# A two-block network's opening: norm's weight applied in rows through a spread on TensorE, h rounded by tiles of tokens, and x's second tile loaded behind the first weights

## What is computed

```
def rmsnorm(x, g):
    xf = x.astype(jnp.float32)
    y = xf * lax.rsqrt(jnp.mean(xf * xf, axis=-1, keepdims=True) + EPS)
    return (y * g.astype(jnp.float32)).astype(x.dtype)
...
    h = rmsnorm(x, norm_mix_g[l])
    proj = jnp.einsum('bsd,dc->bsc', h, w_in[l])
    u, v, bg, cg, xs, ga, gb = jnp.split(proj, split_at, axis=-1)
    v = rmsnorm(jax.nn.gelu(v, approximate=False), norm_v_g[l])
...
    x = x + conv_ffn(h, ffn_w_up[i], ffn_conv_w[i], ffn_conv_b[i], ffn_w_down[i])
return rms_norm(x, final_norm_g)
```

## Time and profile before

| | |
|---|---|
| median of three runs | 1022.09 us (1021.5 to 1022.81) |
| the profiled execution's own time | 1022.21 us |
| its span | 1020.4 us |
| TensorE busy | 1004.5 us, 98% |
| VectorE busy | 760.2 us, 74% |
| ScalarE busy | 572.8 us, 56% |
| first instruction of TensorE | 4.43 us into the span |

### The profile page before, as it was taken

How to read it: one execution, slowest core, us unless ns; L and a number is a source line. 1 busy time by engine, 2 the same in 40 slices (tenths; PEclk the granted TensorE clock), 3 DMA queues, 4 the chain that set the end, 5 groups by cost and what they waited for, 6 DMA issues and landing times.

```text
span 1020.4 us, 18696 instructions
## 1 busy us (share of the span) xinstructions
PE 1004.5 (98%) x7236; PEld 934.2 (92%) x7236; DVE 760.2 (74%) x1015; ACT 572.8 (56%) x817; POOL 6.6 (1%) x20
## 2 busy tenths in 40 slices
PE   7999999999999999999999999999999999999997
PEld 5999999999999999977899999999998898888886
DVE  7676655557766656787878877778878789888886
ACT  7543444445444445557866555555646675666665
POOL 0000000000000000000000000000020000000000
PEclk9999999999999999999999999999999999999999
DMA  8645556456665664454464666674324574666652
GB/s 301 211 154 176 190 200 203 165 168 203 207 198 173 201 208 167 138 198 140 163 188 125 186 185 186 185 211 142 125 63 103 166 226 139 199 190 191 190 162 83
DMA packets 191265, 178.87 MB, mean 175 GB/s; under 512 B 17444, under 2 KB 169586, under 8 KB 191218
## 3 DMA queue, kind: packets, MB, share of 16 engines
q1 hardware_dynamic: 191218, 178.22, 56.3%
HBM read 177.15 MB, written 1.05 MB: 175 GB/s over the span
## 4 chain that ended last, share of the span: by engine, by line
PE 91%; DVE 5%; ACT 2%; DMA 2%; issue 0%; SPq 0%; DVEq 0%; ACTq 0%
PE psum L622 18%; PE psum L624 17%; PE psum L623 17%; PE psum L824 14%; PE psum L826 7%; PE psum L629 4%; PE psum L631 4%; PE psum L630 4%; DVE whl L1751 2%; DMA raw<-da_w_qkv 1%; PE psum L956 1%; ACT whl L1266 1%; PE psum L972 1%; DMA raw<-w_in 1%; PE psum L1204 1%; DVE stat L2133 1%
## 5 line engine op out<-in xcount | busy, mean ns | idle before, releaser
L1751 DVE TENSOR_TENSOR whl<-raw,whl 128x2048 fp32r<-128x2048 f32 (+2 forms) x145 | 298.1, 2062 | 77.5 <-ACT whl L1266 77.0
L1266 ACT ACTIVATE whl<-raw 128x2048 fp32r<-128x2048 f32 (+2 forms) x145 | 248.1, 1716 | 73.6 <-DMA raw<-w_ff 25.8
L622 PE MATMUL psum<-hT,whl 128*128 128x256 f32 (+1 forms) x784 | 220.4, 281 | 0.9 <-DVE hT L1826 0.9
L623 PE MATMUL psum<-hT,whl 128*128 128x256 f32 (+1 forms) x784 | 219.2, 280 | 0.0
L624 PE MATMUL psum<-hT,whl 128*128 128x256 f32 (+1 forms) x784 | 218.5, 279 | 0.0
L824 PE MATMUL psum<-hT,whl 128*128 128x512 f32 x608 | 212.9, 391 | 0.0
L826 PE MATMUL psum<-hT,whl 128*128 128x256 f32 x608 | 171.4, 282 | 0.0
L622 PEld LDWEIGHTS psum<-hT,whl 128*128 128x128 f32 (+1 forms) x784 | 147.1, 188 | 1.5 <-issue 0.7
L623 PEld LDWEIGHTS psum<-hT,whl 128*128 128x128 f32 (+1 forms) x784 | 147.2, 188 | 0.1
L624 PEld LDWEIGHTS psum<-hT,whl 128*128 128x128 f32 (+1 forms) x784 | 147.2, 188 | 0.0
L622 PE MATMUL psum<-lat,whl 128*128 128x256 f32 (+1 forms) x512 | 144.4, 282 | 0.4 <-DVE whl L1751 0.3
(11 more groups left out here) (250 smaller groups left out, 1582.1 us busy)
## 6 DMA issues: line engine op xcount, KB each, us to landing
raw<-w_ff SPq DMA_DIRECT2D x32, 1024.0 KB, 5.6
raw<-w_in SPq DMA_DIRECT2D x24, 1024.0 KB, 5.1
raw<-ffn_w_up SPq DMA_DIRECT2D x44, 512.0 KB, 4.9
q_sb<-ffn_w_up SPq DMA_DIRECT2D x44, 512.0 KB, 5.0
raw<-da_w_qkv SPq DMA_DIRECT2D x12, 1024.0 KB, 5.0
q_sb<-ffn_w_down SPq DMA_DIRECT2D x22, 512.0 KB, 3.7
raw<-ffn_w_down SPq DMA_DIRECT2D x22, 512.0 KB, 3.6
raw<-w_proj_a SPq DMA_DIRECT2D x4, 1024.0 KB, 5.2
```

The lines of the kernel that those rows point to most:

```text
L622: mm(dst, weight(n, 0, cols, kt, c0, m), hi, start=start, stop=False, skip_group_check=True)
L623: mm(dst, weight(n, 0, cols, kt, c0, m), lo, start=False, stop=False, skip_group_check=True)
L1266: fn(whl[:, slot, 0, 0:w], landing(n)[:, 0:w], ACT.Copy).then_inc(hi_ready, 1)
L1751: tt(whl[:, slot, 1, 0:w], landing(n)[:, 0:w], whl[:, slot, 0, 0:w].bitcast(F32), ALU.subtract).then_inc(lo_ready, 1)
```

## The change

- The weight of the norm is loaded as one row of 1024 (`mix_row`) and spread over all 128 partitions by two fp32 matmuls with a row of ones (`unit_row`), into two PSUM banks. VectorE multiplies it in when it scales the rows (`normal_x`, two products of 512 columns for each tile), so that `round_h` and `rest_h` need no scale.
- TensorE turns the scaled rows tile by tile into two banks for each tile (`h_bank`), and `round_h` and `rest_h` work on four blocks of one tile at a time, in the order tile 0 low half, tile 1 low half, tile 0 high half, tile 1 high half (`H_ORDER`).
- Tile 1's transposes of scaled rows stand behind the first six matmuls of v, and the transposes of x's tile 1 behind tile 0 of the second chunk. The deviation of tile 1 comes behind h of tile 0 on ScalarE and VectorE. The copies of tile 0 into `xT` are now ScalarE's.
- SyncE issues the first half chunk ahead of x's tile 1. The column form of the weight is loaded later with the other vectors.
- In `inject_x` the products with the identity are marked as transposes.

```diff
@@ SyncE
-            sp.dma_start(vec_rows[0:KT, 0, :], a["norm_mix_g"].rearrange("l (r c) -> (l r) c", c=P)).then_inc(mix_landed, 16)
-            sp.dma_start(x_rows[:, 1, :], x_in[:, 1, :]).then_inc(x_landed[1], 16)
+            sp.dma_start(mix_row[:], a["norm_mix_g"]).then_inc(mix_landed, 16)
             for n in range(N_MIX):
...
                 sp.dma_start(dst[:, 0:KT // 4, :], src[:, 0:KT // 4, :]).then_inc(half_landed[n], 16)
+                if n == 0:
+                    sp.dma_start(x_rows[:, 1, :], x_in[:, 1, :]).then_inc(x_landed[1], 16)
                 sp.dma_start(dst[:, KT // 4:, :], src[:, KT // 4:, :]).then_inc(rest_landed[n], 16)
...
-            for name, rows in VEC_ROWS[1:]:
+            for name, rows in VEC_ROWS:
@@ TensorE
+        H_ORDER = [(0, 0), (1, 0), (0, 1), (1, 1)]
+        h_bank = ((py, px), (bank[2], bank[3]))
...
+            def turn_x(dst, src, t, ready, done):
+                for kt in range(KT):
+                    if ready is not None and kt % 4 == 0:
+                        pe.wait_ge(ready, 2 * t + kt // 4 + 1)
+                    last = nc.tensor.transpose(flat(dst[kt // 4])[:, kt % 4 * P:(kt % 4 + 1) * P],
+                                               src[:, t, kt * P:(kt + 1) * P], ident)
+                    if kt % 4 == 3:
+                        last.then_inc(done, 1)
...
+            turn_x(bank[0:2], x_rows, 0, None, x_turned)
+            pe.wait_ge(const_set, 2)
             pe.wait_ge(mix_landed, 16)
+            for half in range(2):
+                last = mm(flat(up[half]), unit_row[:], mix_row[:, half * D // 2:(half + 1) * D // 2], start=True, stop=True)
+            last.then_inc(mix_spread, 1)
+            turn_x(h_bank[0], vtok, 0, xn_ready, xn_turned)
@@ v_rows
+                    if n == 0 and at == 0:
+                        pe.wait_ge(x_read, t + 1)
+                    if n == 1 and t == 1 and at == 0:
+                        pe.wait_ge(x_landed[1], 16)
+                        turn_x(h_bank[0], x_rows, 1, None, x_turned)
                     if t == 0 and at == KT // 4:
+                        if n == 0:
+                            turn_x(h_bank[1], vtok, 1, xn_ready, xn_turned)
                         pe.wait_ge(lo_ready, n + 1)
-                    if t == 0 and n < 2:
-                        pe.wait_ge(h_ready, max(2, kt + 1))
+                    if n < 2:
+                        pe.wait_ge(h_ready, 2 * H_ORDER.index((t, n)) + 2)
@@ inject_x
                             mm(token_sum(t, kt // 4)[:, kt % 4 * P:(kt % 4 + 1) * P], xT[:, kt, t * P:(t + 1) * P], ident,
-                               start=kt % 4 == 0, stop=False, skip_group_check=True)
+                               start=kt % 4 == 0, stop=False, is_transpose=True, skip_group_check=True)
@@ ScalarE
-                fn(hT[:, kt, 0, :], bank[kt // 2][:, kt % 2, :], ACT.Identity, scale=mix_g[:, kt:kt + 1]).then_inc(h_hi, 1)
+            def round_h(t, c):
+                act.wait_ge(xn_turned, 2 * t + c + 1)
+                fn(hT[:, 4 * c:4 * c + 4, 0, t * P:(t + 1) * P], of_tiles(h_bank[t][c]), ACT.Copy).then_inc(h_hi, 2)
...
+            x_deviation(0)
             split_hi_half(0, 0)
+            for half in range(2):
+                act.wait_ge(x_turned, half + 1)
+                fn(xT[:, 4 * half:4 * half + 4, 0:P], of_tiles(bank[half]), ACT.Copy).then_inc(x_read, 1)
+            for at in H_ORDER[0:1]:
+                round_h(*at)
+            x_deviation(1)
+            split_hi_half(0, 1)
+            for at in H_ORDER[1:3]:
+                round_h(*at)
             split_hi_half(1, 0)
+            for at in H_ORDER[3:4]:
+                round_h(*at)
             split_hi_half(1, 1)
@@ VectorE
+            def normal_x(t):
+                dve.wait_ge(x_std, t + 1)
+                step.wait(step.mark(nc.vector.reciprocal(xstat[:, 2, t:t + 1], xstat[:, 1, t:t + 1])))
+                dve.wait_ge(mix_spread, 1)
+                for half in range(2):
+                    cols = slice(half * D // 2, (half + 1) * D // 2)
+                    stt(vtok[:, t, cols], x_rows[:, t, cols], xstat[:, 2, t:t + 1], up[half].rearrange("p a b -> p (a b)"),
+                        ALU.mult, ALU.mult).then_inc(xn_ready, 1)
+            normal_x(0)
             split_lo_half(0, 0)
+            for at in H_ORDER[0:1]:
+                rest_h(*at)
+            normal_x(1)
+            split_lo_half(0, 1)
+            for at in H_ORDER[1:3]:
+                rest_h(*at)
             split_lo_half(1, 0)
+            for at in H_ORDER[3:4]:
+                rest_h(*at)
             split_lo_half(1, 1)
```

More of the change, by code:

```diff
@@ L692, in turn_reciprocal @@
                 last.then_inc(r_turned, 1)
-            pe.wait_ge(ident_landed, 16)
-            pe.wait_ge(mix_landed, 16)
-            nc.tensor.transpose(bank[3][:, 0, 0:KT], vec_rows[0:KT, 0, :], ident[0:KT, 0:KT]).then_inc(mix_turned, 1)
-            x_bank = [up[0], up[1], px, py]
-            def turn_x(dst, src, t, done):
-                for kt in range(KT):
-                    last = nc.tensor.transpose(dst[kt // 2][:, kt % 2, t * P:(t + 1) * P],
-                                               src[:, t, kt * P:(kt + 1) * P], ident)
-                    if done is not None and kt % 2 == 1:
-                        last.then_inc(done, 1)
-            pe.wait_ge(x_landed[0], 16)
-            turn_x(x_bank, x_rows, 0, None)
-            pe.wait_ge(mix_g_read, 1)
-            pe.wait_ge(xn_ready, 1)
-            turn_x(bank, vtok, 0, None)
-            pe.wait_ge(xn_ready, 2)
-            turn_x(bank, vtok, 1, xn_turned)
-            pe.wait_ge(x_landed[1], 16)
-            turn_x(x_bank, x_rows, 1, x_turned)
             def flat(b):
                 return b.rearrange("p a b -> p (a b)")
+            x_bank = [up[0], up[1], px, py]
+            def turn_x(dst, src, t, ready, done):
[6 more added lines that the diff above has]
+                        last.then_inc(done, 1)
+            pe.wait_ge(ident_landed, 16)
+            pe.wait_ge(x_landed[0], 16)
+            turn_x(bank[0:2], x_rows, 0, None, x_turned)
+            pe.wait_ge(const_set, 2)
+            pe.wait_ge(mix_landed, 16)
+            for half in range(2):
+                last = mm(flat(up[half]), unit_row[:], mix_row[:, half * D // 2:(half + 1) * D // 2], start=True, stop=True)
+            last.then_inc(mix_spread, 1)
+            turn_x(h_bank[0], vtok, 0, xn_ready, xn_turned)
             def v_rows(n):
@@ L1318, in _, with x_deviation @@
             x_flat = t_act[:].rearrange("p a b c -> p (a b c)")
-            for t in range(TT):
+            def x_deviation(t):
                 act.wait_ge(x_landed[t], 16)
@@ L1325, in _ @@
                 fn(xstat[:, 1, t:t + 1], xstat[:, 0, t:t + 1], ACT.Sqrt, bias=eps[:, 0:1], scale=1.0 / D).then_inc(x_std, 1)
+            x_deviation(0)
             split_hi_half(0, 0)
-            act.wait_ge(mix_g_read, 1)
-            for kt in range(KT):
-                if kt == KT // 2:
-                    split_hi_half(0, 1)
-                round_h(kt)
+            for half in range(2):
[7 more added lines that the diff above has]
+                round_h(*at)
             split_hi_half(1, 0)
+            for at in H_ORDER[3:4]:
+                round_h(*at)
             split_hi_half(1, 1)
@@ L1814, in split_lo_half, with rest_h @@
                    ALU.subtract).then_inc(half_lo if half == 0 else lo_ready, 1)
-            def rest_h(kt):
-                dve.wait_ge(h_hi, kt // 2 * 2 + 2)
-                stt(hT[:, kt, 1, :], bank[kt // 2][:, kt % 2, :], mix_g[:, kt:kt + 1], hT[:, kt, 0, :].bitcast(F32),
-                    ALU.mult, ALU.subtract).then_inc(h_ready, 1)
+            def rest_h(t, c):
+                dve.wait_ge(h_hi, 2 * H_ORDER.index((t, c)) + 2)
+                four, of_t = slice(4 * c, 4 * c + 4), slice(t * P, (t + 1) * P)
+                tt(hT[:, four, 1, of_t], of_tiles(h_bank[t][c]), hT[:, four, 0, of_t].bitcast(F32),
+                   ALU.subtract).then_inc(h_ready, 2)
             def rest_x(k, c, gain):
@@ L1892, in _ @@
                     split_lo(n)
+                if c == 0:
+                    for half in range(2):
+                        dve.wait_ge(x_turned, 3 + half)
+                        copy(xT[:, 4 * half:4 * half + 4, P:2 * P], of_tiles((py, px)[half])).then_inc(x_read, 1)
             dve.wait_ge(v_std, 1)
```

26 lines of the change are left out of this document (8 added, 18 removed).

## The result

The changed kernel takes 1027.39 us (median of six executions, 1026.76 to 1028.12), the kernel before beside it 1021.8 (1020.37 to 1022.81). The ratio is 1.006, with an interval of 1.005 to 1.0069: slower by some 5.6 us. The forecast was 1022.6 with a range up to 1024.2, so the range missed it by over 3 us.

A forecast was written before the change was run, and what follows sets the result against it. TensorE, busy 98% of the span, was taken to bound the kernel. From a median of 1022.09 us, opening +2.05 and injection -1.55 gave 1022.6 us, range 1021.0 to 1024.2.

The forecast's parts named there:

- The landing: Opening transfers: with the issue order swapped, the first half chunk lands near 7.3 us and x's tile 1 near 8.9.
- The spread: TensorE's opening: two fp32 matmuls of 512 columns, four passes, from 6.15 to 8.87 us; VectorE has the weight at 9.07.
- I take the change of pace at 8.15, as in before: Within the spread: TensorE runs at the slow early pace until 8.15 us, then twice as fast.
- The third rival: Opening: the whole spread runs at the early pace, 3.44 us instead of 2.72, 1.15 more, total 1023.8; chance 0.13.
- VectorE's chain: Behind the spread: two products, first weights' rest, rest of h, done at 12.23; v's first matmuls at 12.31 against 12.29.
- The second wait: After tile 1's transposes: TensorE idles from 14.59 until VectorE's second half chunk's rest, resuming at 15.32, 1.18 us later.
- The rest of the stream: The remaining 90 matmuls of v run unstopped, but x's tile 1 transposes stand inside: 0.87 us; opening 2.05 later.
- Behind it ... all shifts together: After the opening: everything that loads or rounds waits for buffers TensorE frees, so all moves by the same amount.
- The injection: Last stage: 16 transposes replace 32 passes, 1.83 us less, of which a wait for weights takes back 0.28: 1.55 less.
- The fourth rival: Opening: TensorE falls back to the lower clock level, resuming 1.5 us past 15.32, total 1024.4; chance 0.09.
- The rule that I set beside the earlier trace: Opening: transposes do not bring the full clock, so the whole spread would run at half the clock.

The follow-up runs named there:

- after_aligned: Changed kernel with mix_g's old place kept as a hole and unit_row moved, so aT, cT and mT lie as in before: 1023.82 us, ratio 1.0027.
- before_again: The kernel before, no edit, profiled a second time: 1023.1 us, one execution.
- before_shifted: The kernel before with 480 unused bytes per partition behind mix_g, so later tiles lie further off: 1023.68 us against 1020.79, ratio 1.0029.
- after_dma_aligned: Changed kernel with the norm's weight spread by its transfer instead of TensorE, tiles at their old places: 1024.77 us, one execution.
- before_turns: The kernel before with only the injection's 16 products marked as transposes: 1019.62 us against 1020.54, ratio 0.999.
- before_turns_more: The kernel before with only the injection's products as transposes, run again in more rounds: 1019.44 us against 1021.26, ratio 0.9981.
- the filled kernels: Kernels with unread ones-products in TensorE's opening gaps; longer attention stage in before with transposed injection (1021.25 us) and the changed kernel with 128-row spread, old places (1022.44).
- after_pad: Changed kernel with 32 unused bytes behind unit_row, so what follows lies 512 bytes further than in before, not 480: 1024.19 us, one execution.
- after_filled: Changed kernel with old tile places and unread ones-products filling TensorE's opening gaps, spread still over one row: 1023.0 us, ratio 1.0026.
- after_filled_rows128: Changed kernel with old tile places, gaps filled by ones-products and the spread over 128 rows: 1020.91 us, one execution, beside a before of 1020.56.

## Why the prediction failed, step by step

- **The landing** held. The first half chunk was to land near 7.3; ScalarE starts on it at 7.03.
- **The spread** failed by its pace: 6.15 to 9.03 forecast, last result included, 6.25 to 10.03 measured. The step at fault is "I take the change of pace at 8.15, as in before". That was one execution, and five profiles of that opening range from 8.2 to 16.1; the change then takes away what TensorE had to do there and puts in the one-row matmuls and longer waits. The third rival held this spread (3.44 us), but let the pace rise four transposes behind it.
- **VectorE's chain** held in its lengths: products 1.41 for two, 1.32 to the next instruction (10.15 to 11.47), the weights' rest 1.22. The products and the first weights' rest were shifted by 1.08. The transposes at 0.2 held up ScalarE and so the rest of h, and the start of v came 1.39 later than forecast.
- **The second wait** was taken from the wrong engine. Forecast: six matmuls in 1.40, eight transposes in 0.88, then 0.73 of waiting for VectorE until 15.32. Measured: six in 2.70, eight in 1.56, and no wait at 17.96, since the weights' rest was done at 15.68 + 1.22 = 16.90. The slower TensorE had become the bound. From the start of v to the other 90 matmuls it took 4.26, where I had 3.01.
- **The rest of the stream**: 22.27 us from 17.96 to 40.23, against 21.11 in before. x's transposes cost 0.80 of that (25.36 to 26.16; forecast 0.87), the two slow matmuls at the start of the 90 another 0.41 (17.96 to 18.84, where two take 0.47). The three pieces make 4.98 instead of 2.05.
- **"Behind it ... all shifts together"** failed. It holds for the order of work, but not for the place of the tiles in memory, which no step of mine looked at. This is the larger miss, 3.4 us against 2.93 in the opening, and it was on no list of rivals. The code of before gave a sign: two tiles of 32 bytes that nothing uses, `half_line` (L254) and `half_line_m` (L288, right ahead of `mT`).
- **The injection** held: 1.46 less against 1.55. It is 1.82 shorter (forecast 1.83), and what was given back is one wait of 0.24 (forecast 0.28), at the very matmul of the forecast, now at 863.67, and 0.11 behind it, where the next start follows 0.34 later instead of 0.23.

Added up, the two profiles differ by 5.36 where the forecast had 0.50. The 4.86 between them are 2.93 in the opening, 3.40 from the place of the tiles, 0.09 in the last stage and 0.11 on the way to the second sum, less the 1.67 that do not belong to the change.

The fourth rival, a fall to the lower level in the opening, was nearest in its outcome (1024.4) and got 0.09; in fact the level was not lost in after, it had never come. What it lost is the same: slow matmuls of v, slow transposes of tile 1. Without the new memory place the changed kernel stands 3.0 above the before of its own comparison (after_aligned, 1023.82 against 1020.79), where the range reached 2.1 above; so the opening alone would have put the time a little outside, and the place of the tiles put it far outside.

The rule that I set beside the earlier trace rows, from the Trainium skill, "TensorE: Matmul & The Clock Gate", section "Part 4: PE-mode transpose", says that transposes do not count as matmuls do for the full clock. I wrote that the trace disagrees. Over the runs that was too strong: in before_again, before_shifted and after_dma_aligned the level comes only with the matmuls of v, at 16.1, 14.4 and 18.6, and in before, before_turns and before_turns_more behind transposes alone, at 8.2, 8.3 and 13.0, ahead of the first matmul of v. One trace could not carry a verdict on it.

What stays open: why the level comes at such different times in one and the same program, why a place 480 bytes on makes matmuls slower, the stage of 188.5 against 186.9 us, and the longer attention stage of the filled kernels.

## What to carry to other kernels

A new tile of another size moves all that is allocated behind it; compare the mean length of untouched matmuls before and after, and keep the old size as a hole if they differ. An opening in which TensorE has little to do is read from several executions, since the time at which its clock rises differs among them, and work that seems free there is costed at the slow pace. A change of several parts is split: here some 1.5 us of gain (products with the identity as transposes) lay hidden under 7 us of loss, and alone it beats the kernel before, 1019.44 us against 1021.26.

## What the runs showed of the hardware

- A matmul of 256 columns takes 283 ns by its record, and 0.120 us between starts, when the tile whose 256 columns it reads lies 480 bytes further (after, before_shifted), and 279 ns and 0.117 us at the old place or 512 bytes on (before, after_aligned, after_pad). The granted clock reads 1.00 in both. The stage with 576 of them takes 2.35 us more, of which they make 1.9.
- With the gaps filled, the granted clock falls at 8.2 us behind 1.9 us of fp32 matmuls that contract over one row, and does not fall behind the same sums over 128 rows (after_filled, after_filled_rows128, one profile each). TensorE is busy for 2.00 and 1.98 of the 2.00 us from 8 on.
- A transpose by `is_transpose` of fp32 takes one pass where the product with the identity takes two: 16 passes in 1.67 us against 32 in 3.49, both at a granted clock of 1.00.
